# Layer norms' statistics in PSUM, sums moved between VectorE and GpSimd, vector products turned, in a two-block model kernel

## The reference

```python
def hybrid_layer(x, ...):
    h = x @ w_in                                  # three mixers on its columns
    mix = concatenate([o_sb, o_mla, o_rwkv]) @ w_o
    x = layer_norm(DEEPNORM_ALPHA * x + mix, ln1_g, ln1_b)
    u_act, u_gate = split(x @ ffn_w_up, 2)
    hid = gelu(causal_depthwise_conv(u_act)) * u_gate
    return layer_norm(DEEPNORM_ALPHA * x + hid @ ffn_w_down, ln2_g, ln2_b)

def layer_norm(x, g, b):
    mu = mean(x); var = mean(square(x - mu))
    return (x - mu) * rsqrt(var + LN_EPS) * g + b
```

## Time and profile before

| | us |
|---|---|
| median of 3 runs | 2384.37 (2382.88 to 2385.79) |
| the profiled execution, its own time | 2383.53 |
| its span in the profile | 2381.7 |
| PE busy | 2309.4 (97%) |
| DVE busy | 1450.3 (61%) |
| ACT busy | 1028.9 (43%) |
| POOL busy | 276.2 (12%) |
| stages of k = 0 (start): mixers' half, ahead pair, turned pair, next | 315.8, 338.9, 360.8, 374.6 |
| ahead pair of k = 1, 2, 5 (start) | 714.7, 1051.1, 1628.8 |

### The profile page before, as it was taken

One profiled execution on the slowest core, in us unless ns is written; L12 is line 12 of the kernel. 1 busy time (PEld: TensorE's weight loads), 2 busy tenths in 40 slices (PEclk: granted clock), 3 DMA queues, 4 the chain that ended last, 5 costly groups with the idle time before them and its releaser, 6 DMA issues.

```text
span 2381.7 us, 35746 instructions
## 1 busy us (share of the span) xinstructions
PE 2309.4 (97%) x13360; PEld 1856.7 (78%) x13360; DVE 1450.3 (61%) x1970; ACT 1028.9 (43%) x1603; POOL 276.2 (12%) x199
## 2 busy tenths in 40 slices
PE   8999999999999999999999998999999999999998
PEld 6777767888887777767888876778888888888887
DVE  4668678666577678688666556577444356443443
ACT  5667245333345667245333334665233243332332
POOL 0042221000042141220000040201000010000001
PEclk9999999999999999999999997999999999999999
DMA  4210014555432210014555431222322221223222
GB/s 162 80 62 28 29 45 159 194 194 193 162 106 82 87 54 28 29 45 168 197 191 193 159 109 36 80 94 94 106 96 94 94 96 62 89 97 97 97 97 88
DMA packets 68797, 248.33 MB, mean 104 GB/s; under 512 B 7632, under 2 KB 8144, under 8 KB 68688
## 3 DMA queue, kind: packets, MB, share of 16 engines
q1 hardware_dynamic: 68688, 246.85, 31.1%
HBM read 244.72 MB, written 2.10 MB: 104 GB/s over the span
## 4 chain that ended last, share of the span: by engine, by line
PE 48%; DVE 4%; ACT 2%; issue 1%; DVEq 0%; ACTq 0%
PE dense L668 15%; PE dense L669 14%; PE dense L670 14%; PE aux L853 1%; PE aux L668 1%; ACT wh L1538 1%; PE aux L669 1%; PE aux L670 1%; DVE wl L2361 1%; DVE xc L3116 0%; DVE xc L3083 0%; DVE xc L3082 0%; DVE xc L3081 0%; PE aux L1483 0%; DVE hidl L2396 0%
## 5 line engine op out<-in xcount | busy, mean ns | idle before, releaser
L1538 ACT ACTIVATE wh<-raw 128x1024 fp32r<-128x1024 f32 x338 | 358.0, 1059 | 866.9 <-PE dense L670 858.4
L668 PE MATMUL dense<-xh,wh 128*128 128x512 f32 x1712 | 685.1, 400 | 16.4 <-DVE wl L2361 11.5
L2361 DVE TENSOR_TENSOR wl<-raw,wh 128x1024 fp32r<-128x1024 f32 x338 | 427.1, 1264 | 410.7 <-ACT wh L1538 408.8
L670 PE MATMUL dense<-xh,wl 128*128 128x512 f32 x1712 | 668.0, 390 | 0.0
L669 PE MATMUL dense<-xl,wh 128*128 128x512 f32 x1712 | 667.5, 390 | 0.0
L668 PEld LDWEIGHTS dense<-xh,wh 128*128 128x128 f32 x1712 | 322.1, 188 | 104.1 <-issue 25.9
L669 PEld LDWEIGHTS dense<-xl,wh 128*128 128x128 f32 x1712 | 322.4, 188 | 69.4 <-issue 5.8
L670 PEld LDWEIGHTS dense<-xh,wl 128*128 128x128 f32 x1712 | 321.8, 188 | 68.0
L668 PE MATMUL dense<-hidh,wh 128*128 128x512 f32 x928 | 362.9, 391 | 4.9 <-DVE hidl L2396 2.1
L669 PE MATMUL dense<-hidl,wh 128*128 128x512 f32 x928 | 361.2, 389 | 0.0
L670 PE MATMUL dense<-hidh,wl 128*128 128x512 f32 x928 | 361.2, 389 | 0.0
(11 more groups left out here) (445 smaller groups left out, 2745.0 us busy)
## 6 DMA issues: line engine op xcount, KB each, us to landing
raw<-stream SPq DMA_DIRECT2D x362, 512.0 KB, 3.4
mraw<-mod_stream SPq DMA_DIRECT2D x96, 512.0 KB, 4.3
x<-x_t SPq DMA_DIRECT2D x4, 512.0 KB, 7.0
y_t<-x SPq DMA_DIRECT2D x8, 256.0 KB, 2.0
cst<-consts SPq DMA_DIRECT2D x1, 993.0 KB, 9.3
band<-bands SPq DMA_DIRECT2D x1, 576.0 KB, 4.4
cond<-c_rows SPq DMA_DIRECT2D x1, 512.0 KB, 10.6
pv_next<-vecs SPq DMA_DIRECT2D x3, 82.5 KB, 4.5
```

The lines of the kernel that those rows point to most:

```text
L668: pe.matmul(o, a, h, start=first, stop=False)
L670: return pe.matmul(o, b, h, start=False, stop=last)
L1538: act.activation(wh[:, slot].rearrange("p k m -> p (k m)"), raw[:, slot, :], ACT.Copy).then_inc(hi_done, 1)
L2361: tt(wl[:, slot].rearrange("p k m -> p (k m)"), raw[:, slot, :], wh[:, slot].rearrange("p k m -> p (k m)").bitcast(F32), SUB)\
```

## The change

1. **Mean and deviation.** ScalarE writes rstd to aux4 (`RSTD`), and VectorE's centre and scale read the sum and rstd from aux5 (`MEAN`) and aux4. The mean is still copied to mean_t, and its square is made from that. At k = 5 rstd is written twice, to aux4 and to rstd_t.
2. **Sums at k = 0, 2.** VectorE adds x in aux3 (`tile_sum`) and the squares in aux4, the last addition of each going to norm_sum and norm_sq in SBUF. GpSimd makes the low parts of four chunks there (`low_weights`: the last two of W_o and the first two of the FFN), which VectorE's `refill` made.
3. **Vector products.** At the end of each half, not after each tile, vcol's columns are the stationary operand and both chunks' weights (256 columns) move; both chunks are released together then (+2). The result lies in rows; ScalarE copies it (`rows_out`), and TensorE turns it back by two matmuls after tile 3 of the turned pair (`vector_columns`).
4. **Banks.** `TURNED` is aux3 and dense1. The chunk behind the turned pair in dense1 now waits for all readings of that bank before it (the `+ 2 * j`).
5. **Order.** ScalarE makes the second halves of the turned pair's weights after tiles 1 and 2 (before: 0 and 2), VectorE after 2 and 3 (before: 1 and 3), with four centres ahead of the variance (before: three) and six in all ahead of the first scale (before: five), and both early halves behind it.
6. Some semaphores are merged.

The core of the diff:

```diff
         OUT_ORDER = (2, 0, 1, 3)
         MODS = 24
-        AHEAD, TURNED, COLS = (aux[0], aux[1]), (aux[3], aux[4]), aux[2]
+        AHEAD, TURNED, COLS = (aux[0], aux[1]), (aux[3], dbank[1]), aux[2]
+        MEAN, RSTD = aux[5], aux[4]
 
         def mod_late(L):
...
 
-                if k in (0, 2) and square:
-                    pe.wait_ge(sq_added, sq_sums_before(k) + 7)
+                if k in (0, 2):
+                    pe.wait_ge(sq_added, sq_sums_before(k) + (14 if square else 13))
                 elif k < 4 and square:
                     pe.wait_ge(sq_added, sq_sums_before(k) + 8)
                 else:
...
-                            split_product(AHEAD[j][:], ((s + j) % 2, t * P), slice(0, P),
-                                          (h[:, t, :], l[:, t, :]), t == 0, t == KT - 1)
-                            m = pe.matmul(COLS[:, 8 * j:8 * j + n_hi], wh[:, (s + j) % 2, t, :],
-                                          vcol[:, t, mine], start=t == 0 and j == 0, stop=False,
-                                          skip_group_check=True)
+                            m = split_product(AHEAD[j][:], ((s + j) % 2, t * P), slice(0, P),
+                                              (h[:, t, :], l[:, t, :]), t == 0, t == KT - 1)
                             if j == 1 and k in IN_PLACE:
                                 m.then_inc(tile_used, 1)
-                            m = pe.matmul(COLS[:, 8 * j:8 * j + 2], wl[:, (s + j) % 2, t, :],
-                                          vcol[:, t, ours], start=False, stop=t == KT - 1,
-                                          skip_group_check=True)
-                        m.then_inc(pe_half if half == 0 else pe_chunk, 1)
                         if half == 0 and j == 0 and k < 4:
                             spread(k, False)
+                    m = vector_rows(k, half)
+                    m.then_inc(pe_half if half == 0 else pe_chunk, 2)
                     if half == 0:
                         spread(k, True)
 
-            def turned_pair(pl, s, n, tile):
+            def vector_rows(k, half):
+
+                mine = slice(0, 4) if k < 4 else slice(1, 4, 2)
+                n = 4 if k < 4 else 2
+                for t in range(4 * half, 4 * half + 4):
+                    pe.matmul(COLS[0:n, 0:2 * P], vcol[:, t, mine], wh[:, :, t, :],
+                              start=t == 0, stop=False)
+                    m = pe.matmul(COLS[0:2, 0:2 * P], vcol[:, t, mine][:, 0:2], wl[:, :, t, :],
+                                  start=False, stop=t == KT - 1)
+                return m
+
+            def vector_columns(k):
+
+                pe.wait_ge(rows_read, deferred_before(k) + 1)
+                n, ones = (4, const("fold", slice(0, 4))) if k < 4 else \
+                    (2, const("ones", slice(0, 2), 2))
+                for j in range(2):
+                    m = pe.matmul(COLS[:, 256 + 2 * j:258 + 2 * j], rows_t[0:n, P * j:P * j + P],
+                                  ones, start=j == 0, stop=True, skip_group_check=True)
+                m.then_inc(cols_pe, 1)
+
+            def turned_pair(pl, s, n, k, tile):
 
                 q = halves(n)
                 for t in range(KT):
                     tile(t)
+                    if t == 3:
+                        vector_columns(k)
                     for j in range(2):
...
                             pe.wait_ge(lo_half, 2 * q + j + 1)
+                            if j == 1:
+                                pe.wait_ge(bank_free[1], pl.use(s + 1) - 1)
                         if t == 4:
                             pe.wait_ge(lo_done, pl.chunk(s + j) + 1)
...
                 for j in range(2):
                     pe.wait_ge(lo_half, 2 * (q + 1) + j + 1)
-                    pe.wait_ge(bank_free[j], pl.use(s + j, 1) - 2)
+                    pe.wait_ge(bank_free[j], pl.use(s + j, 1) - 2 + 2 * j)
...
                 ahead_pair(pl, s, n, k)
-                turned_pair(pl, s + 2, n, tile)
+                turned_pair(pl, s + 2, n, k, tile)
...
                 act.wait_ge(mean_pe, k + 1)
-                act.activation(mean_t[:], aux[5][:], ACT.Copy, scale=1.0 / D)\
-                    .then_inc(mean_ready, 1)
-                act.activation(var_t[:], aux[5][:], ACT.Square, scale=1.0 / D)\
-                    .then_inc(mean_ready, 1)
+                act.activation(mean_t[:], MEAN[:], ACT.Copy, scale=1.0 / D).then_inc(mean_ready, 1)
+                act.wait_ge(mean_ready, 2 * k + 1)
+                act.activation(var_t[:], mean_t[:], ACT.Square).then_inc(mean_ready, 1)
 
             def root_stats(k):
 
                 act.wait_ge(var_ready, k + 1)
                 act.activation(var_t[:], var_t[:], ACT.Ln).then_inc(sd_ready, 1)
                 act.wait_ge(sd_ready, k + 1)
-                act.activation(rstd_t[:], var_t[:], ACT.Exp, scale=-0.5).then_inc(rstd_ready, 1)
+                act.activation(RSTD[:], var_t[:], ACT.Exp, scale=-0.5).then_inc(rstd_ready, 1)
+                if k == 5:
+                    act.activation(rstd_t[:], var_t[:], ACT.Exp, scale=-0.5)\
+                        .then_inc(rstd_copied, 1)
+
+            def rows_out(k):
+
+                n = 4 if k < 4 else 2
+                act.activation(rows_t[0:n, :], COLS[0:n, 0:2 * P], ACT.Copy).then_inc(rows_read, 1)
 
...
 
-            def between(pl, s, q, m):
-
-                if m in (0, 2):
-                    rest(pl, s + m // 2)
+            def between(pl, s, q, m, k):
+
+                if m in (1, 2):
+                    rest(pl, s + m - 1)
+                    if m == 2:
+                        rows_out(k)
...
                     dve.wait_ge(mean_ready, 2 * k + 1)
-                tt(x[:, m, :], x[:, m, :], mean_t[:], SUB).then_inc(centred_x, 1)
+                stt(x[:, m, :], MEAN[:], -1.0 / D, x[:, m, :], MUL, ADD).then_inc(centred_x, 1)
...
+                    chain(dve.tensor_copy(small[:, 12, 0:4], COLS[:, 256:260]))
+                    if also is not None:
+                        tt(small[:, 12, 4:5], small[:, 12, 1:2], also, MUL)
                 if k < 4:
-                    for n in range(2):
-                        t = column(v, n, 8 * j + n, 8 * j + 2 + n)
-                    chain(t)
-                    if also is not None:
-                        tt(v[:, 2:3], v[:, 1:2], also, MUL)
...
                 else:
-                    column(v, 1, 8 * j, 8 * j + 1)
+                    if j == 0:
+                        dve.wait_ge(rstd_copied, 1)
                     tt(ahead_t[:, j, :], AHEAD[j][:], rstd_t[:], MUL).then_inc(ahead_ready, 1)
 
-            def column(v, n, a, b):
-
-                return ts(v[:, n:n + 1], COLS[:, a:a + 1], COLS[:, b:b + 1], None, ADD)
-
             def between(pl, s, q, m):
 
-                if m in (1, 3):
-                    rest(pl, s + m // 2)
+                if m in (2, 3):
+                    rest(pl, s + m - 2)
                 elif m >= 6:
                     early_half(q + 1, m - 6)
 
             def turned_tiles(k, g, b, pl, s, q):
 
-                early_half(q, 0)
-                for m in range(3):
+                lead = 6
+                for m in range(4):
                     centre(k, m)
                 variance_tile(k)
-                early_half(q, 1)
-                lead = 5
-                for m in range(3, lead):
+                for j in range(2):
+                    early_half(q, j)
+                for m in range(4, lead):
                     centre(k, m)
                 dve.wait_ge(rstd_ready, norms_scaled(k) + 1)
 
...
+                def tile_sum(m):
+
+                    if m > 1:
+                        dve.wait_ge(sq_added, sq_sums_before(k) + 2 * m - 3)
+                    dve.wait_ge(*x_added(k, m))
+                    tt(norm_sum[:] if m == KT - 1 else aux[3][:], x[:, m, :],
+                       x[:, 0, :] if m == 1 else aux[3][:], ADD).then_inc(sq_added, 1)
+
                 def square_sum(m):
 
                     dve.wait_ge(sq_ready, 8 * k + m + 1)
                     if m > 1:
-                        dve.wait_ge(sq_added, sq_sums_before(k) + m - 1)
-                    tt(norm_sq[:], sq[:, 0, :] if m == 1 else norm_sq[:], sq[:, m % 2, :], ADD)\
-                        .then_inc(sq_added, 1)
+                        dve.wait_ge(sq_added, sq_sums_before(k) + 2 * m - 2)
+                    tt(norm_sq[:] if m == KT - 1 else aux[4][:], sq[:, m % 2, :],
+                       sq[:, 0, :] if m == 1 else aux[4][:], ADD).then_inc(sq_added, 1)
 
...
                             dve.wait_ge(pe_chunk, pl.chunk(C_WO + 4 + a) + 1)
                         m = 2 * a + e
                         tt(x[:, m, :], x[:, m, :], dbank[e][:], ADD).then_inc(bank_free[e], 1)
-                        if e and (ahead or a < 3):
-                            refill(pl, C_WO + 4 + a)
                         if m >= 2:
                             square_sum(m - 1)
-                        if ahead and m:
```

(13 more changed lines are left out.)

98 lines of the change are left out of this document (47 added, 51 removed).

## The result

| | kernel before | changed kernel |
|---|---|---|
| median, us (range) | 2383.05 (2379.18 to 2385.79), 14 runs | 2389.30 (2387.05 to 2391.46), 14 runs |
| ratio | | 1.0029, 95% interval 1.0022 to 1.0036 |
| span of the profiled execution, us | 2381.7 | 2389.5 |

The change costs 6 to 7 us. The forecast was 2386 against 2384.4, that is 1.6 us more: the sign was right and the size a quarter of it. The page of the changed kernel shows little of this: TensorE is again busy for 97%, and stands idle for 79.3 us where it was 72.3.

What follows compares the result with a forecast made beforehand. TensorE, busy for 97% of the span, bounds the kernel, with VectorE and GpSimd where it waits. Gains of 18.2 us, 0.3 more and 19.5 lost make +1.6 us on a median of 2384.37: 2386 us, range 2372 to 2400.

Steps and rivals of the forecast that it cites:

- The new wait: Behind the turned pairs, the next chunk in dense1 waits for its reading: 4.2 + 4.2 + 5.1 + 1.9 = 15.4 us lost.
- Slow clock behind the waits: Three of the four waits for dense1 lower TensorE's clock: 1.8 + 1.8 + 1.4 = 5.0 us lost, between nought and 9.
- Sums: Ahead pair at k=0 and k=2: the 2.70 us wait for the mean goes, with 3.0 us of slow clock at k=0.
- VectorE keeps up: Mixers' half, k=0 and 2: eight VectorE operations of about 0.65 us, 5.2 us per chunk against TensorE's 5.44.
- the rules against it: Low parts with both inputs in SBUF could wait for all of a GpSimd 128x1024 subtraction; 5.2 us per chunk becomes 7.3.
- rival b: GpSimd bounds the mixers' half, from about 2.9 us per 128x1024 operation; 2398 us at 3.3, slower; chance 0.22.
- only matmuls can be saved: At k=1 and k=5 TensorE doesn't wait in the ahead pair, so only its matmul time can shrink.
- k=5: Gain of 1.0 us there: 1.84 less the columns, a second copy of the deviation and VectorE's chain.
- Turned pair: At k=0, 13.8 us becomes 13.2, 0.6 less, with 0.35 for turning rows back; bounds 11.2 and 14.2.
- Vector products: Each stage: 16 matmuls of 256 columns, 0.12 us apart, take 1.92 us instead of 3.76, saving 1.84 us.
- Rival d: Vector products with 4 stationary and 256 moving columns take a full 0.227 us each; 2393 us, slower; chance 0.06.
- Rivals c and e: First: dense1 waits don't lower the clock, 2377 us, chance 0.22. Second: no wait for dense1, 2366 us, chance 0.05.

Runs made afterwards that it cites:

- The bank alone: The kernel before with only the turned pair's second product put in dense1, whose next chunk waits for its reading: 2405.03 us, ratio 1.0083.
- the one with 5, 7, 5 and 0 matmuls: The changed kernel with 5, 7, 5 and 0 unread matmuls filling the wait for dense1 at k=0, 1, 2, 5: 2385.99 us, ratio 1.0016.

## Why the mean still waits: a lock

The forecast had the mean's sum ready at 25.2 us from the start of the half, with no wait; it was there at 26.7. VectorE's low parts and GpSimd's subtractions in the changed kernel, by line (shortest, median and longest in ns), and the longest one in the timeline:

```profile
L2476 DVE SCALAR_TENSOR_TENSOR hidl<-x,pv,hidh x16: 739/1192/2892, 325.0 to 1062.3; 128x512 fp32r<-128x512 f32 x16
...
L3361 POOL TENSOR_TENSOR wl<-raw,wh x8: 2358/2402/2475, 324.8 to 1058.9; 128x1024 fp32r<-128x1024 f32 x8
```
```profile
324.95 2.89 DVE L2476 SCALAR_TENSOR_TENSOR hidl<-x,pv,hidh 128x512 fp32r<-128x512 f32 x1
```

One started at 324.95, 0.13 us after GpSimd's subtraction (324.82, 2.48 us), and ended 0.55 us behind it, where its own time is 0.74. Eight of the sixteen started during a subtraction: they took 1.64 to 2.89 us, and every one ended 0.54 or 0.55 us behind it. The other eight took 0.74. Residuals and both sums, with a PSUM operand, are at 673 to 699 ns throughout. To see whether it is the operands, the low parts of tiles 0 to 5 got the running sum in PSUM for the high part in SBUF:

```diff
+                if k in (0, 2) and m < 6:
+                    dve.wait_ge(sq_added, sq_sums_before(k) + 2 * m + 1)
-                stt(l[:, m, :], x[:, m, :], gain, h[:, m, :].bitcast(F32), MUL, SUB)\
+                stt(l[:, m, :], x[:, m, :], gain,
+                    aux[3][:] if k in (0, 2) and m < 6 else h[:, m, :].bitcast(F32), MUL, SUB)\
```

> The changed kernel, but at k=0 and k=2 the low parts of tiles 0 to 5 read the running sum in aux3 in place of the high part in SBUF, so that they have one operand in SBUF (the low parts are then not those of x). Theory 2 (GpSimd's subtraction holds the shared port for its whole 2.4 us, and VectorE's low part waits for it, which makes the mean's sum late): low parts of tiles 0 to 5 at 0.74 us and none at 1.7 to 2.9, idle time ahead of the mean's spread 1.05 to under 0.3 us, 2 to 3 us less in all, 2387. Rival (the low parts are long because of something else, or the mean waits for ScalarE's squares): idle time stays at 1 us.

Measured: 2386.41 us (2381.51 to 2388.19, 11 runs), ratio 1.0007 (0.9998 to 1.0016), against 1.0029 for the changed kernel.

The low parts by line, the mean's spread in the timeline, and the windows of the mixers' half and the ahead pair:

```profile
L2478 DVE SCALAR_TENSOR_TENSOR hidl<-x,pv,aux x12: 746/748/750, 325.2 to 1054.0; 128x512 fp32r<-128x512 f32 x12
```
```profile
342.48 0.59 PE L777 MATMUL aux<-norm_sum,cst 128*128 128x512 f32 x1
```
```profile
317.89:339.76 21.87, 21.87 (x97) 18.12 (x98) 17.09 (x27) 12.34 (x21) 7.39 (x4) 1.00 0.25 77
339.76:354.66 14.90, 14.82 (x69) 10.76 (x67) 14.12 (x22) 7.22 (x12) 2.38 (x1) 1.00 0.19 64
```

All twelve take 746 to 750 ns, six of them beside a subtraction, and the spread of the mean follows without a wait. The low part of tile 6, left as it was, took 2.33 us in the same run and again ended 0.55 us behind the subtraction. Theory 2 holds: with both inputs in SBUF the operation stood still for the rest of GpSimd's. This agrees with the Trainium skill, "SBUF — State Buffer", section "Who interferes with whom", which has a lock for the whole instruction. The two stages take 36.8 us here against 38.8 in the changed kernel, 0.9 us less in the mixers' half and 1.1 in the ahead pair, and as much at k=2: so the stretched low parts cost at least 4 us of the execution, more than the wait for the mean alone shows.

A cheap remedy was tried on the version with aux5: the tile's sum ahead of the square's.

```diff
-                        if m >= 2:
-                            square_sum(m - 1)
                         if m:
                             tile_sum(m)
+                        if m >= 2:
+                            square_sum(m - 1)
+                        if m:
                             ahead_lo(k, m - 1, vec("ln1_g", m - 1))
```

> The kernel with the second product of the turned pair in aux5 (2369.9), with VectorE adding a tile to the mean's sum ahead of the square's, not behind it. Theory 2: the idle time ahead of the mean's spread at k=0 and k=2 falls from 1.05 us by one operation, 0.6, to 0.45; 1.2 us less, 2368.7. Rival (squares become late instead): an idle time of 0.5 us or more ahead of the squares' spread and no gain.

Measured: 2369.90 us (2368.75 to 2371.85, 5 runs), ratio 0.9944 (0.9931 to 0.9958): no gain. The wait for the mean is 0.80 us, not 0.45, and an earlier one grew from 0.56 to 1.35:

```profile
330.47 2.75 DVE L2474 SCALAR_TENSOR_TENSOR hidl<-x,pv,hidh 128x512 fp32r<-128x512 f32 x1
...
333.88 0.50 PE L673 MATMUL dense<-xh,wh 128*128 128x512 f32 x1 [1.35 <-DVE x L3011]
...
343.18 0.70 PE L777 MATMUL aux<-norm_sum,cst 128*128 128x512 f32 x1 [0.80 <-DVE norm_sum L2993]
```

With another order a low part of 2.75 us stands right ahead of a residual, which comes late instead. Of the rival the missing gain came true, but at another place than the squares' spread.

## Why the prediction was right, and where it was short

- **The new wait** carried the sign. 15.4 us were forecast and 15.8 measured, by reading when a bank that nobody had waited for was read before. The bank alone, in the kernel before, gave the waits and 21 us.
- **Slow clock behind the waits**: 5.0 forecast, 7.2 by the start times, within the bounds of nought and 9. The single waits were taken at 1.4 to 1.8 and measured at 2.1 to 2.8. That k=5's wait leaves the clock alone was right in this profile and in two others with that wait; in the fourth, the one with 5, 7, 5 and 0 matmuls, the clock fell behind it.
- **Sums** (2.70, 3.0 and 1.7 of clock at k=0 and k=2): the wait and the clock went, but 1.05 and 1.01 us of wait stayed where nought was forecast. The step that failed is "VectorE keeps up": eight operations of 0.65 us per chunk, with nothing for the low parts that wait for GpSimd. The forecast named this wait under the rules against it, gave it a share of rival b's chance and put its cost in the sum at nothing; measured, it is 2.0 us at each of k=0 and k=2. GpSimd's 2.4 us for 128x1024 was 2402 ns, so rival b's condition (2.9) was not met; its mechanism came in a different form, in VectorE's queue.
- **k=1**: 2.1 forecast, 1.2 measured. TensorE, 0.85 us earlier at the spread, now waits 0.97 for GpSimd's last addition, a wait that "only matmuls can be saved" left out:

```profile
719.79 0.70 PE L777 MATMUL aux<-norm_sum,cst 128*128 128x512 f32 x1 [0.97 <-POOL norm_sum L3371]
```

- **k=5**: 1.0 forecast, 0.3 measured. The ahead pair gave 1.15 instead of 1.84, mostly since TensorE now stands idle for 0.36 us ahead of its second chunk, until VectorE has made that chunk's low weight. The turned pair went from 11.03 to 11.9 us. It is 11.89 us with the vector products alone too, so it is they that cost this, and not the second copy of the deviation. The two matmuls that turn the rows back were taken at 0.35 us; from the last matmul ahead of them to the first behind them the starts are 0.84 us apart, where two matmuls in a row have 0.23:

```profile
1652.85 0.39 PE L675 MATMUL dense<-xh,wl 128*128 128x512 f32 x1
1653.16 0.60 PE L821 MATMUL aux<-cst,rows_t 2*128 2x2 f32 x4
1653.69 0.50 PE L673 MATMUL aux<-xh,wh 128*128 128x512 f32 x1
```

- **Turned pair** at k=0: 13.2 forecast, 13.30 measured, by luck in part: two terms were mis-sized and cancel. The products make it 0.8 to 0.9 us longer, not 0.35, and the deviation in PSUM makes it 1.3 shorter.
- **Vector products**: 0.12 us apart, as forecast:

```profile
348.41 0.28 PE L809 MATMUL aux<-wh,vcol 128*4 128x256 f32 x1
...
348.52 0.28 PE L811 MATMUL aux<-wl,vcol 128*2 128x256 f32 x1
```

Rival d falls. But the saving of 1.84 us a stage was counted in full, and at k=0, 1 and 2 the part of it in half 0 goes into the wait for the mean.
- **Rivals c and e** fall by the slow windows and the rows of the four waits.

- **k=3**: 0.3 us more forecast, 0.5 less measured. Its cause was not looked for.

So the losses behind the turned pairs were sized fairly well (19.5 us forecast, 21.8 measured) and the gains were taken 4.5 us too high. Together that is 6.8 us, a little more than the 6.2 by which the spans' 7.8 exceeds 1.6.

The sign itself is worth less than it looks. A sum of +1.6 us from two halves of 18 and 19.5, each with an error of 3 to 5 us by the forecast's own words, could have had either sign. It lay inside the 4.8 us that the forecast called no change, to which it gave the highest chance, 0.39. The measured 6.3 us is slower by that line, which had 0.34, mostly for rivals b and d, and neither came true as it was put. What was forecast in earnest, and came, is the four waits.

## What to carry to other kernels

Before a result is put into a bank that the next chunk uses, find the time of its last reading in the old trace and subtract the time at which that chunk starts. That difference was the wait here, to within 0.1 us at all four places, and the queue paid it in full, with the clock on top at three of them. A saving on an engine counts only from the point where that engine doesn't wait for something else; look at what is late next in each stage, for an earlier arrival can just lengthen the old wait. When two products' releases are put together, look through every queue for what stands behind the instruction that waits for them.

## What the runs showed of the hardware

- The same idle time doesn't always have the same effect on the clock. Behind the wait of 1.79 us near 1585 the clock stayed at 1.00 in seven of the twelve profiles, as in the kernel before, and was low in five, with a loss of 1.6 us; here that of the kernel with the mean first:

```profile
1568.90:1572.30 3.40, 3.35 (x11) 2.71 (x12) 3.40 (x6) 1.24 (x2) 0.00 (x0) 0.73 0.46 154
```

  Behind the wait of 2.9 us near 1519 it was low in ten of twelve, and not in that of the vector products alone, nor in that of the sums alone:

```profile
1509.60:1515.50 5.90, 5.59 (x23) 4.29 (x24) 1.23 (x1) 5.90 (x10) 2.93 (x2) 1.00 0.22 77
```

  Behind the waits of 4.1 to 5.4 us for dense1 it was low all nine times. So chance in a single profile's clock is worth 1 to 3 us, the size of several terms of the sum.
- A GpSimd subtraction of 128x1024 takes 2402 ns where the 128x512 one takes 1287 at least: nearly twice.
- A VectorE operation of 0.74 us with two SBUF inputs took up to 2.89 us when it started during such a subtraction, always ending 0.54 or 0.55 us behind it, and never over 0.75 with one of them in PSUM.
